# The x part of the SSD's causal convolution: from turned channels to tokens on partitions, with four shifted loads

## The reference, cut to what matters

```python
out = conv(u, w, padding=[(3, 0)], feature_group_count=channels) + b   # causal, 4 taps
xbc = silu(out)
xs, Bm, Cm = split(xbc, (4096, 1024, 1024))
y = ssd_chunked(xs, dt, A, Bm, Cm)      # needs x with tokens on partitions, B and C with channels on partitions
y = y + D * xs
```

## Time and profile before

| what | value |
|---|---|
| median of 3 runs | 2899.79 us (2899.49 to 2900.23) |
| the profiled execution | 2899.11 us, span 2897.8 us, granted clock 0.999 |
| PE / DVE / ACT / POOL busy | 99% / 61% / 51% / 3% of the span |
| bytes moved | 632.07 MB, mean 218 GB/s |
| 12 transposes at L696, per group | one block of 12 between two matmuls of the stream |
| 8 transposes at L712, per group | one block of 8 |

### The profile page before, as it was taken

One profiled execution on the slowest core, in us unless ns is written; L12 is line 12 of the kernel. 1 busy time (PEld: TensorE's weight loads), 2 busy tenths in 40 slices (PEclk: granted clock), 3 DMA queues, 4 the chain that ended last, 5 costly groups with the idle time before them and its releaser, 6 DMA issues. The chain is left out here.

```text
span 2897.8 us, 34839 instructions
## 1 busy us (share of the span) xinstructions
PE 2878.1 (99%) x13590; PEld 2395.9 (83%) x13590; DVE 1770.8 (61%) x2276; ACT 1480.3 (51%) x2054; POOL 82.5 (3%) x126
## 2 busy tenths in 40 slices
PE   9999999999999999999999999999999999999998
PEld 8888888888888788888888888888888888888887
DVE  5567666666655555567655545555666656676546
ACT  5456666665555554544443434434555555645544
POOL 0000000000000000000000000000000011000010
PEclk9999999999999999999999999999999999999999
DMA  7766776667766677775665665756586666766665
GB/s 244 256 199 225 232 230 224 234 227 239 263 221 217 233 227 255 260 266 157 234 196 171 206 182 175 212 180 196 164 277 198 215 202 214 236 228 220 216 217 177
DMA packets 330243, 632.07 MB, mean 218 GB/s; under 512 B 27773, under 2 KB 47037, under 8 KB 329054
## 3 DMA queue, kind: packets, MB, share of 16 engines
q1 hardware_dynamic: 270976, 510.33, 54.7%
q10 hardware_dynamic: 46350, 75.36, 8.1%
q0 software_dynamic: 12752, 44.15, 4.4%
HBM read 580.06 MB, written 49.69 MB: 217 GB/s over the span
## 5 line engine op out<-in xcount | busy, mean ns | idle before, releaser
L1661 DVE TENSOR_TENSOR w_lo<-raw,w_hi 128x1024 fp32r<-128x1024 f32 (+1 forms) x979 | 1157.8, 1206 | 673.0 <-ACT w_hi L1027 661.8
L995 PE MATMUL bank<-w_lo,x_hi 128*128 128x512 f32 (+2 forms) x3888 | 1527.5, 393 | 3.1 <-issue 2.0
L997 PE MATMUL bank<-w_hi,x_lo 128*128 128x512 f32 (+2 forms) x3888 | 1508.3, 388 | 0.0
L996 PE MATMUL bank<-w_hi,x_hi 128*128 128x512 f32 (+2 forms) x3888 | 1506.6, 388 | 0.0
L1027 ACT ACTIVATE w_hi<-raw 128x1024 fp32r<-128x1024 f32 (+1 forms) x979 | 992.8, 1044 | 688.1 <-PE bank L997 237.9
L995 PEld LDWEIGHTS bank<-w_lo,x_hi 128*128 128x128 f32 x3888 | 730.4, 188 | 152.1 <-issue 7.0
L997 PEld LDWEIGHTS bank<-w_hi,x_lo 128*128 128x128 f32 x3888 | 729.9, 188 | 150.8
L996 PEld LDWEIGHTS bank<-w_hi,x_hi 128*128 128x128 f32 x3888 | 730.7, 188 | 146.4 <-issue 2.6
L1032 ACT ACTIVATE x_hi<-bank 128x512 fp32r<-128x512 f32 (+1 forms) x104 | 57.3, 588 | 294.6 <-PE bank L624 294.5
L1666 DVE TENSOR_TENSOR x_lo<-bank,x_hi 128x512 fp32r<-128x512 f32 (+1 forms) x104 | 67.1, 676 | 178.8 <-ACT x_hi L1032 178.8
L2387 POOL DMA_DIRECT2D proj<-stage x60 | 43.5, 725 | 2520.3 <-DVE stage L2262 1597.4
(11 more groups left out here) (220 smaller groups left out, 1291.5 us busy)
## 6 DMA issues: line engine op xcount, KB each, us to landing
raw<-in_w_in SPq DMA_DIRECT2D x496, 512.0 KB, 5.0
raw<-in_w_up SPq DMA_DIRECT2D x128, 512.0 KB, 4.3
raw<-in_w_down SPq DMA_DIRECT2D x128, 512.0 KB, 4.7
raw<-in_w_out SPq DMA_DIRECT2D x96, 512.0 KB, 4.8
raw<-in_w_ssd_branch SPq DMA_DIRECT2D x64, 512.0 KB, 5.6
proj<-stage POOLq DMA_DIRECT2D x60, 512.0 KB, 5.7
arena<-proj ACTq DMA_DIRECT2D x50, 512.0 KB, 4.7
raw<-in_w_gla_branch SPq DMA_DIRECT2D x32, 512.0 KB, 5.4
```

Source lines behind the costliest of these rows:

```text
L995: pe.matmul(o, x_hi[:, xk, tokens(t)], w_lo[:, r, k, 0:b.n], start=a, stop=False)
L996: pe.matmul(o, x_hi[:, xk, tokens(t)], w_hi[:, r, k, 0:b.n], start=False, stop=False)
L997: op = pe.matmul(o, x_lo[:, xk, tokens(t)], w_hi[:, r, k, 0:b.n], start=False, stop=z_)
L1661: TT(w_lo[:, p % SPLIT_RING, 0:b.per, 0:b.n], raw[:, p % RAW_RING, 0:b.per, 0:b.n], w_hi[:, p % SPLIT_RING, 0:b.per, 0:b.n].bitcast(F32), ...
```

## The change: what it does

The DRAM tensor `proj` gets three rows ahead of token 0; POOL fills their 6144 conv columns with zeros at the start (three DMAs of 24 KB). For x, the group loads four tiles of 256 tokens by 512 channels, each one row later than the one before, with tokens on partitions (`tap_u`), and beside each its row of weights sent to all partitions (`tap_w`, 256 KB); two slots serve the four taps. The bias row (`tap_b`, 256 KB) comes the same way. DVE multiplies and adds in `xt`, and ACT applies SiLU in place. B and C are turned and convolved as before.

PE does 4 transposes at "u" instead of 12 and none at "x". The steps of the group become: taps 0 and 1 at +4 and +6, a new ACT step "later" at +8 that issues the loads of taps 2 and 3, taps 2 and 3 at +10 and +12, and "z", "x", "y", "off", "out" two places later each (12, 14, 18, 21, 25).

```diff
-CONV_T = 6
+CONV_T = 2
+TAP_RING = 2
-SSD_STEP = {"load": 0, "u": 3, "dec": 6, "cb": 8, "z": 10, "x": 12, "y": 16, "off": 19, "out": 23}
+SSD_STEP = {"load": 0, "u": 3, "taps": (4, 6, 10, 12), "later": 8, "dec": 6, "cb": 8, "z": 12, "x": 14, "y": 18, "off": 21, "out": 25}
...
+    before_proj = scratch("proj", [CONV_W - 1 + S, N_IN])
     dram = {
-        "proj": scratch("proj", [S, N_IN]),
+        "proj": before_proj[CONV_W - 1:, :],
...
 # PE, step "u"
-            for n in (2, 0, 1):
-                for c in (2 * n, 2 * n + 1):
-                    for t in range(NT):
-                        op = pe.transpose(bank[CONV_BANK[n]][:, (c % 2) * S + t * P:(c % 2) * S + (t + 1) * P],
-                                          uin[:, t, c * P:(c + 1) * P], ident[:, :])
-                op.then_inc(*ssd.pe("u", g, n))
+            for c in range(CONV_T):
+                for t in range(NT):
+                    op = pe.transpose(bank[4][:, c * S + t * P:c * S + (t + 1) * P], uin[:, t, c * P:(c + 1) * P],
+                                      ident[:, :])
+            op.then_inc(*ssd.pe("u", g))
...
 # PE, step "x": gone
-            for t in range(NT):
-                for c in range(4):
-                    op = pe.transpose(bank[5 + t][:, c * P:(c + 1) * P], cv[:, c, tokens(t)], ident[:, :])
-                op.then_inc(*ssd.pe("x", g, t))
...
 # ACT, step "load": B and C first, then cw and dec as before, then
+            def taps(w):
+                slot = w % TAP_RING
+                act.dma_start(tap_u[:, slot, :, :], rows(before_proj[w:w + S, :])[
+                    :, :, COL_XBC + g * CH:COL_XBC + (g + 1) * CH]).then_inc(*taps_in[slot](g, w))
+                act.dma_start(tap_w[:, slot, :], row_of(i["taps"][g, w], CH)).then_inc(*taps_in[slot](g, w))
+            act.dma_start(tap_b, row_of(i["taps"][g, CONV_W], CH)).then_inc(*taps_in[0](g, "bias"))
+            taps(0)
+            taps(1)
...
 # ACT, step "later" (in the place of the SiLU of x's four turned tiles)
+            yield SSD_STEP["later"]
+            act.wait_ge(*ssd.dve["tap", g, 0])
+            taps(2)
+            act.wait_ge(*ssd.dve["tap", g, 1])
+            taps(3)
...
 # ACT, step "x"
+            act.wait_ge(*ssd.dve["tap", g, CONV_W - 1])
+            for t in range(NT):
+                A(xt[:, t, :], xt[:, t, :], ACT.Silu).then_inc(*ssd.act("xt", g, t))
...
 # DVE
+            def tap(w):
+                slot = w % TAP_RING
+                u, by = tap_u[:, slot, :, :], wide(tap_w[:, slot, :].unsqueeze(1), [P, NT, CH])
+                dve.wait_ge(*taps_in[slot][g, w])
+                if w:
+                    TT(u, u, by, ALU.mult).then_inc(*ssd.dve("product", g, w))
+                    dve.wait_ge(*ssd.dve["product", g, w])
+                    dve.wait_ge(*ssd.dve["tap", g, w - 1])
+                    TT(xt, xt, u, ALU.add).then_inc(*ssd.dve("tap", g, w))
+                    return
+                if g > SSD_UPPER:
+                    dve.wait_ge(*side_out["heads_y", g - 1])
+                elif g:
+                    dve.wait_ge(*ssd.pe["out", g - 1, NT - 1])
+                TT(xt, u, by, ALU.mult).then_inc(*ssd.dve("product", g, 0))
+                dve.wait_ge(*ssd.dve["product", g, 0])
+                TT(xt, xt, wide(tap_b.unsqueeze(1), [P, NT, CH]), ALU.add).then_inc(*ssd.dve("tap", g, 0))
...
 # POOL, at the start
+        pool.wait_ge(*start.dve["zeros"])
+        for r in range(CONV_W - 1):
+            pool.dma_start(before_proj[r, COL_XBC:COL_XBC + SSD_IN].rearrange("(a n) -> a n", n=P),
+                           drained[0:SSD_IN // P, 1, 0, 0:P]).then_inc(*zeros_out(r))
```

More of the change, by code:

```diff
@@ L80 @@
 DEC_PARTS = tuple((t, hb) for t in range(NT) for hb in range(2))
-CONV_BANK = (4, 5, 6)
 SSD_UPPER = 4
@@ L455, in emit @@
     ident_in = tally("ident_in", 16)
+    zeros_out = tally("zeros_out", 16)
+    taps_in = [tally(f"taps{n}_in", 16) for n in range(TAP_RING)]
     mix_in = [tally(f"mix{n}_in", 16) for n in range(2)]
@@ L514, in emit @@
     uin = room(NT, CONV_T * P)
+    tap_u, tap_w = room(TAP_RING, NT, CH), room(TAP_RING, CH)
+    tap_b = room(CH)
     z = room(NT, CH)
@@ L692, in ssd_group @@
             pe.wait_ge(*load[0]["ssd", g])
-            for n in (2, 0, 1):
-                for c in (2 * n, 2 * n + 1):
-                    for t in range(NT):
-                        op = pe.transpose(bank[CONV_BANK[n]][:, (c % 2) * S + t * P:(c % 2) * S + (t + 1) * P],
-                                          uin[:, t, c * P:(c + 1) * P], ident[:, :])
-                op.then_inc(*ssd.pe("u", g, n))
+            for c in range(CONV_T):
[3 more added lines that the diff above has]
+            op.then_inc(*ssd.pe("u", g))
             yield SSD_STEP["cb"]
-            pe.wait_ge(*ssd.act["conv", g, 5])
-            pe.wait_ge(*ssd.act["u", g, 0])
+            pe.wait_ge(*ssd.act["conv", g, 1])
+            pe.wait_ge(*ssd.act["u", g])
             for t in range(NT):
-                pe.matmul(bank[4][:, tokens(t)], cv[:, 4, tokens(t)], cv[:, 5, tokens(t)], start=True, stop=True)
-            pe.matmul(bank[4][:, S:S + P], cv[:, 4, 0:P], cv[:, 5, P:2 * P], start=True, stop=True).then_inc(
+                pe.matmul(bank[4][:, tokens(t)], cv[:, 0, tokens(t)], cv[:, 1, tokens(t)], start=True, stop=True)
+            pe.matmul(bank[4][:, S:S + P], cv[:, 0, 0:P], cv[:, 1, P:2 * P], start=True, stop=True).then_inc(
                 *ssd.pe("cb", g))
-            yield SSD_STEP["x"]
-            pe.wait_ge(*ssd.act["conv", g, 3])
-            for t in range(NT):
-                for c in range(4):
-                    op = pe.transpose(bank[5 + t][:, c * P:(c + 1) * P], cv[:, c, tokens(t)], ident[:, :])
-                op.then_inc(*ssd.pe("x", g, t))
             yield SSD_STEP["y"]
@@ L1091, in ssd_group @@
                 act.wait_ge(*ssd.dve["squares", g - 1, 0])
-            act.dma_start(uin[:, :, 0:CH], proj[:, :, COL_XBC + g * CH:COL_XBC + (g + 1) * CH]).then_inc(
-                *load[0]("ssd", g))
             at = COL_BC + g * P
-            act.dma_start(uin[:, :, CH:CH + P], proj[:, :, at:at + P]).then_inc(*load[0]("ssd", g))
+            act.dma_start(uin[:, :, 0:P], proj[:, :, at:at + P]).then_inc(*load[0]("ssd", g))
             at += SSD_G * SSD_N
-            act.dma_start(uin[:, :, CH + P:CH + 2 * P], proj[:, :, at:at + P]).then_inc(*load[0]("ssd", g))
+            act.dma_start(uin[:, :, P:2 * P], proj[:, :, at:at + P]).then_inc(*load[0]("ssd", g))
             act.dma_start(flat(cw), i["conv"][g]).then_inc(*load[0]("ssd", g))
@@ L1101, in ssd_group @@
                 *load[2]("ssd", g))
[L1103 to L1107, removed]
-            yield SSD_STEP["u"]
[L1110 to L1120, removed]
+            def taps(w):
[6 more added lines that the diff above has]
+            taps(1)
+            yield SSD_STEP["u"]
+            act.wait_ge(*ssd.pe["u", g])
+            if g == 0:
+                act.wait_ge(*ssd.dve["zeros"])
+            A(ut[:, :, CONV_W - 1:], bank[4][:, :].rearrange("p (a b) -> p a b", a=CONV_T), ACT.Copy).then_inc(
+                *ssd.act("u", g))
+            act.wait_ge(*ssd.act["u", g])
+            act.wait_ge(*load[0]["ssd", g])
+            for c in range(CONV_T):
+                A(cv[:, c, :], ut[:, c, 0:S], ACT.Copy, scale=cw[:, c, 0:1]).then_inc(*ssd.act("first", g, c))
+            for c in range(CONV_T):
+                act.wait_ge(*ssd.dve["conv", g, CONV_W - 1, c])
+                A(cv[:, c, :], cv[:, c, :], ACT.Silu, bias=cw[:, c, CONV_W:CONV_W + 1]).then_inc(
+                    *ssd.act("conv", g, c))
             yield SSD_STEP["dec"]
@@ L1132, in ssd_group @@
                 A(some, some, ACT.Exp, scale=-1.0).then_inc(*ssd.act("dec", g, t, hb))
-            yield SSD_STEP["cb"]
-            conv((0, 1, 2, 3))
+            yield SSD_STEP["later"]
[3 more added lines that the diff above has]
+            taps(3)
             act.wait_ge(*ssd.pe["cb", g])
@@ L1147, in ssd_group @@
             yield SSD_STEP["x"]
[L1148 to L1151, removed]
+            act.wait_ge(*ssd.dve["tap", g, CONV_W - 1])
             for t in range(NT):
-                act.wait_ge(*ssd.pe["x", g, t])
-                A(xt[:, t, :], bank[5 + t][:, :], ACT.Copy).then_inc(*ssd.act("xt", g, t))
+                A(xt[:, t, :], xt[:, t, :], ACT.Silu).then_inc(*ssd.act("xt", g, t))
             yield SSD_STEP["y"]
@@ L1565, in result @@
                 act.wait_ge(*summed[b.last])
+                act.wait_ge(*zeros_out[CONV_W - 2])
                 A(drained[0:b.n, b.half, 0, 0:S], bank[2 * b.half][0:b.n, 0:S], ACT.Copy).then_inc(
@@ L1750, in conv @@
                             ALU.add).then_inc(*ssd.dve("conv", g, w, c))
-            yield SSD_STEP["u"]
[L1753 to L1757, removed]
+            def tap(w):
[15 more added lines that the diff above has]
+                TT(xt, xt, wide(tap_b.unsqueeze(1), [P, NT, CH]), ALU.add).then_inc(*ssd.dve("tap", g, 0))
```

(14 more changed lines are left out.)

## The result

| | before | after |
|---|---|---|
| median | 2899.62 us (2899.25 to 2900.23, 5 runs) | 2885.02 us (2883.77 to 2886.38, 5 runs) |
| the profiled execution | 2899.11 us, span 2897.8 | 2886.38 us, span 2885.0 |
| moved by DMA | 632.07 MB | 655.09 MB |

The ratio of the runs is 0.995 with a 95% interval of 0.9935 to 0.9964: faster by 14.6 us, to 2885.0, where 14.0 and 2885.8 were forecast. The profiled execution is the slowest of the five, 12.7 us under its counterpart.

What follows compares the result with a forecast made beforehand. PE, busy in 99% of the span, was taken as the bound. 8 groups at 1.75 us save 14.0 us: 2899.11 to 2885.1 profiled, with the median 0.7 above, 2885.8 us; range 2882.5 to 2893.8.

Steps and rivals of the forecast that it cites:

- PE's room: PE's stream at "u" and "x": 1.75 us less per group, 14.0 us in 8 groups, 0.11 us per transpose.
- rival C: Each of the 128 transposes on PE saves its whole 272 ns: 34.8 us, to 2865.0 us; chance 0.03.
- The leads: Group 5's weights stay ready ahead of PE, by 1.5 us at +11 and +13, 2.1 at +15; none used up.
- the loads' late start: Groups 1 to 4: loads of +0 start some 10 us ahead of "u" instead of 15; bounds nothing to 1 us stall.
- small stalls: Up to 3 us of small stalls set against the mechanism's saving of 12.7 to 14.3 us in its range.
- rival A: Leads of 1.5 us at +11 and +13 used up, PE waits 1.0 us in 8 groups: 2893.8 us; chance 0.17.
- The tap loads: Group 5's loads of taps 2 and 3 issued near 568 to 570, tap 2 landing at 574 to 576.
- rival B: DVE stands at +10 for tap 2's load, PE waits 2.9 us: 9 us slower, 2909 us; chance 0.10.
- The lower end of the range: 2882.5 us for the whole kernel, called all that the PE rows can give.

Runs made afterwards that it cites:

- experiment 1: The changed kernel with all 128 transposes put back on PE, 8 more at "u" and 8 at "x" in each group: 2898.67 us.
- experiment 3: The changed kernel with only the 8 transposes a group at "x" put back on PE: 2891.44 us.
- experiment 6: The changed kernel with one more load of 512 KB a group among the loads of step 0: 2889.08 us.
- experiment 4: The changed kernel with the loads of taps 2 and 3 issued at step 12 instead of 8: 2946.73 us.

## Why the prediction was right

- **PE's room.** "u" 1.32 to 0.44, "x" 0.87 to nothing: both as taken from the rows, 14.0 us. Measured 14.6 by medians, 12.7 by the two profiled executions, 13.65 by putting the transposes back, 6.4 for the half of them. This term carried the whole result. That the median came within 0.8 us is in part luck: undisturbed groups gave 1.84 us and not 1.75 (14.7 in 8; where the 0.09 comes from is open), and the small waits of groups 1 to 3 took 1.4 back. The whole duration as a price (rival C, 34.8 us) is excluded by experiments 1 and 3.
- **The leads.** Walked for group 5, they came within 0.6 us: +11 done 1.6 ahead of PE (1.5 walked), +13 1.9 (1.5), +15 2.7 (2.1), tap 2 started by DVE 24.8 us behind "u" (25.3 walked, from 549.6). The operations over 128 x 1024 took 1.22 us, the value taken.
- **A step that was off.** I walked one group and took the others from it. Already before, group 5 was not the closest: in groups 0 and 4 the lead at +11 was 0.1 us and not 0.6. Group 4's rows, one fence each:
```profile
491.15 2.36 DVE L1661 TENSOR_TENSOR w_lo<-raw,w_hi 128x1024 fp32r<-128x1024 f32 x2 [2.68 <-ACT w_hi L1027]
```
```profile
492.50 0.43 PE L995 MATMUL bank<-w_lo,x_hi 128*128 128x512 f32 x1
```
In group 4 the change made the lead 1.2 us. For groups 1 to 4 I had named the loads' late start, and looked for its price at B, C and `cw` ("a stall of 1 us"). Those were never late. What came late were the weights of +9 and +10, which stand behind the same burst, and this used up the lead at +11 in groups 1 to 3. It cost 1.4 us from start to start, of which the profile counts 0.3 as a wait. That is inside the 3 us of small stalls that the range allowed for, but rival A was nearer than its 0.17 tells; one more load of 512 KB made its waits appear (experiment 6).
- **The tap loads.** Walked at 568 to 570, that is 19 us behind "u"; they went out 14.3 behind it. ACT's queue issued them while five of its operations were still to run. This gave a reserve of 4 us or more that the sum did not count on, and for rival B it meant that it was further off than its condition said: only four places later did it come true.
- **Rival B's price.** 2.9 us of waiting counted as 2.9 us. Experiment 4 shows that a wait of some 5 us costs 2 more in clock, and experiment 6 that one of 2.1 us costs 1.9 more. By an estimate from experiment 4, 8 x (2.9 + 2.1 - 1.75), its 9 us would have been about 26; a wait of 2.9 us was not measured.
- **The lower end of the range.** 2882.5 was called all that the PE rows can give, and it is not: 14.3 us off 2899.79 is 2885.5. The measured 2885.0 lies 0.5 below that, less than its runs differ among themselves.

## What to carry to other kernels

Where PE has no idle time, price what you take off it from start to start in the timeline, not by its duration: 0.11 us against 0.27 for a transpose here. Then check by hand, for each kind of group and not for one, how long ahead of PE its inputs are ready, and which transfers share the DMA engines with them. A wait that does reach PE costs more than the idle time that the profile counts: 0.26 us counted were 0.52 from start to start. It costs far more once the granted clock falls.

## What was not expected of the hardware

- ACT's queue issues a DMA ahead of operations that stand before it in the program: the tap loads went out at 556.03 with three Exps (0.6 each) and two conversions (1.0 each) still to run. The trace of before has it too, so the walk could have used it. Where fewer operations are waiting the same issues hold the engine: nine in a row at step 0 left ACT idle for 5.3 us in group 1 (issue of the last at 227.56, next conversion at 228.28). One of the nine took 2.34 us instead of 0.5, which is 1.8 of the 5.3.
- A table load does not wait with the activation behind it: 543.90 to 545.2, then 0.90 us of waiting for DVE.
- TensorE's clock fell to the lower level after single waits of 2.07 us and of 3.8 to 7.3 us, and not after 0.66; beyond the counted wait that cost about 2 us each time, in experiment 4 and in 6.
